# Gate weights loaded in a row, and their column sums moved, in a two-block transformer kernel (one core)

## The reference, cut to what matters

```python
mod = silu_c @ w_mod[l] + b_mod[l]
sh1, sc1, gt1, sh2, sc2, gt2 = jnp.split(mod[:, None, :], 6, axis=-1)
...
h = modulate(rms_norm_2(x, g_pre1[l]), sh1, sc1)
...
x = x + gt1 * rms_norm_2(mix, g_post1[l])
h2 = modulate(rms_norm_2(x, g_pre2[l]), sh2, sc2)
x = x + gt2 * rms_norm_2(ec_moe(h2, ...), g_post2[l])
```

## Time and profile before

| | us |
|---|---|
| median of 3 runs | 2412.12 |
| lowest, highest | 2410.62, 2414.21 |
| the profiled execution | 2412.12 |
| its span | 2410.3 |
| PE busy | 1846.0 |
| DVE busy | 528.3 |
| ACT busy | 286.5 |

### The profile page before, as it was taken

The page is one execution under the profiler, slowest core; times in us unless marked ns, Lnnn a source line. Parts: engine busy times, 40 slices in busy tenths (PEclk is TensorE's granted clock), DMA queues, the critical chain, the costliest instruction groups (busy, mean ns, idle before and its releaser), DMA issues.

```text
span 2410.3 us, 24072 instructions
## 1 busy us (share of the span) xinstructions
PE 1846.0 (77%) x10310; PEld 1025.8 (43%) x10310; DVE 528.3 (22%) x1129; ACT 286.5 (12%) x709; POOL 57.9 (2%) x95
## 2 busy tenths in 40 slices
PE   6999998999998999975766666666666666666665
PEld 3767785767785677543222222222222222222221
DVE  1244322244323337743100010000000000100001
ACT  1113211113211012311000000000000000000001
POOL 1000000000001200100000000000000000000000
PEclk9999999999999999996877787878788777887887
DMA  8843542444454231384999999999999999999997
GB/s 292 249 157 140 195 160 96 155 170 144 162 221 141 96 140 35 117 325 161 386 421 423 422 422 422 423 422 422 422 423 423 422 422 423 423 422 423 423 422 294
DMA packets 150032, 714.81 MB, mean 297 GB/s; under 512 B 11801, under 2 KB 16345, under 8 KB 96431
## 3 DMA queue, kind: packets, MB, share of 16 engines
q1 hardware_dynamic: 144064, 697.08, 72.1%
q10 hardware_dynamic: 3591, 10.29, 1.2%
q0 software_dynamic: 2272, 5.90, 1.1%
HBM read 709.43 MB, written 3.80 MB: 296 GB/s over the span
## 4 chain that ended last, share of the span: by engine, by line
PE 49%; DMA 41%; DVE 5%; ACT 1%; issue 1%; SPq 1%; POOL 0%; DVEq 0%; ACTq 0%
DMA arena<-in_w_up_dram 34%; PE banks L810 14%; PE banks L2380 6%; DMA arena<-in_w_down_dram 4%; PE banks L1663 4%; PE banks L900 3%; PE banks L1672 3%; PE banks L908 2%; PE banks L2407 2%; DMA arena<-in_w_mods_dram 2%; PE banks L815 2%; PE banks L2349 1%; PE banks L928 1%; PE banks L1705 1%; PE banks L956 1%
## 5 line engine op out<-in xcount | busy, mean ns | idle before, releaser
L2380 PE MATMUL banks<-arena 128*32 128x512 f32 (+2 forms) x3072 | 466.8, 736 | 301.3 <-DMA arena<-in_w_up_dram 295.5
L2380 PEld LDWEIGHTS banks<-arena 128*32 128x32 f32 x3072 | 127.5, 136 | 581.3 <-issue 574.7
L810 PE MATMUL banks<-arena 128*128 128x256 f32 x1536 | 344.6, 380 | 4.0 <-DMA arena<-in_w_in_dram 2.5
L810 PEld LDWEIGHTS banks<-arena 128*128 128x128 f32 x1536 | 286.7, 190 | 46.3 <-issue 4.9
L2407 PE MATMUL banks<-arena 128*32 128x512 f32 x1280 | 211.5, 795 | 121.0 <-DMA arena<-in_w_down_dram 74.8
L2520 DVE SCALAR_TENSOR_TENSOR arena<-arena,banks 64x512 f32<-64x512 f32 (+1 forms) x48 | 30.5, 635 | 780.6 <-ACT arena L2432 779.7
L2407 PEld LDWEIGHTS banks<-arena 128*32 128x32 f32 x1280 | 45.8, 129 | 266.0 <-issue 264.6
L2432 ACT ACTIVATE arena<-banks 64x512 f32<-64x512 f32 (+1 forms) x48 | 26.7, 556 | 829.3 <-PE banks L2380 823.4
L1663 PE MATMUL banks<-arena 128*128 128x256 f32 x512 | 118.9, 392 | 3.5 <-DVE arena L1991 1.9
L1663 PEld LDWEIGHTS banks<-arena 128*128 128x128 f32 x512 | 99.6, 197 | 19.0 <-issue 5.2
L2527 DVE COPY arena<-banks 128x512 f32<-128x512 f32 x16 | 11.1, 692 | 376.4 <-PE banks L2415 376.4
(11 more groups left out here) (325 smaller groups left out, 1623.9 us busy)
## 6 DMA issues: line engine op xcount, KB each, us to landing
arena<-in_w_gate_dram SPq DMA_DIRECT2D x128, 1376.0 KB, 30.1
arena<-in_w_up_dram SPq DMA_DIRECT2D x128, 1376.0 KB, 31.9
arena<-in_w_down_dram SPq DMA_DIRECT2D x160, 1024.0 KB, 30.4
arena<-in_w_in_dram SPq DMA_DIRECT2D x68, 1024.0 KB, 7.5
arena<-in_w_mods_dram SPq DMA_DIRECT2D x48, 1024.0 KB, 7.3
arena<-in_w_out_dram SPq DMA_DIRECT2D x12, 1024.0 KB, 5.7
arena<-in_w_down_dram SPq DMA_DIRECT2D x16, 512.0 KB, 21.8
arena<-in_w_o_swa_dram SPq DMA_DIRECT2D x4, 1024.0 KB, 10.9
```

Of the source, the lines that this page charges most:

```text
L810: mm = pe.matmul(b[:, i * S:i * S + S], w, rhs[:, kt, :], start=kt == 0, stop=kt == 7)
L2380: mm = pe.matmul(bank[pc][32 * g:32 * g + 32, 0:w_], xsT[:, kt, CAP * e4:CAP * e4 + CAP], (wg if g < 2 else wu)[:, c:c + w_], start=kt == ...
```

## The change

It puts all four gate loads of a stage together: in the layers behind `qb` and ahead of `kb`, in the second block behind `kn` and ahead of `vn`, and the last gate behind the four `mod` chunks. The DVE sums move with them: in the layers half 1 behind the lambda sums and half 2 behind the mean squares; in the second block both halves behind `xT2`; for the last gate half 1 behind head 1 of the scan and half 2 behind head 2. The `gate` jobs come earlier in PE's order in the layers, `gate2` comes ahead of `rk`, and `vc` 0 ahead of `v` 1. No new function is called.

```diff
     chunk("w_in", D, COL["qb"], 512)
+    for r in (0, 512):
+        for c in (4, 5):
+            loads.append(("mods_now", r, 4, 512 * c, 512))
     chunk("w_in", D, COL["kb"], 256)
-    for c in (4, 5):
-        loads.append(("mods_now", 0, 4, 512 * c, 512))
     loads.append(("w_uq", 0, 2, 0, MLA_H * QK))
     chunk("w_in", D, COL["qc"], 512)
     loads.append(("w_ukv", 0, 1, 0, MLA_H * (NOPE + VD)))
-    for c in (4, 5):
-        loads.append(("mods_now", 512, 4, 512 * c, 512))
...
     jobs += [("rotk", 0, ()), ("q", 0, uq), ("q", 1, uq), ("qc", 0, qc), ("rotq", 0, ()),
-             ("q", 2, uq), ("q", 3, uq), ("qc", 1, qc), ("rotq", 1, ()), ("kn", 0, ukv), ("kn", 1, ukv),
-             ("kc", 0, kc), ("rotq", 2, ()), ("kn", 2, ukv), ("kn", 3, ukv), ("kc", 1, kc), ("rotq", 3, ()), ("v", 0, ukv), ("v", 1, ukv), ("gate", 0, ()),
-             ("vc", 0, vc), ("gate", 1, ()), ("vc", 1, vc)]
+             ("q", 2, uq), ("q", 3, uq), ("gate", 0, ()), ("qc", 1, qc), ("rotq", 1, ()), ("kn", 0, ukv), ("kn", 1, ukv),
+             ("gate", 1, ()), ("kc", 0, kc), ("rotq", 2, ()), ("kn", 2, ukv), ("kn", 3, ukv), ("kc", 1, kc), ("rotq", 3, ()), ("v", 0, ukv), ("vc", 0, vc),
+             ("v", 1, ukv), ("vc", 1, vc)]
...
-        if name in ("kn", "vn"):
-            for c in (4, 5):
-                loads.append(("mods_now", 0 if name == "kn" else 512, 4, 512 * c, 512))
+        if name == "kn":
+            for r in (0, 512):
+                for c in (4, 5):
+                    loads.append(("mods_now", r, 4, 512 * c, 512))
+        for m in MODS_AFTER.get(name, ()):
+            for r in (0, 512):
+                loads.append(("w_mods", r, 4, 512 * m, 512))
         if name in MODS_AFTER:
             for r in (0, 512):
                 for c in (4, 5):
                     loads.append(("w_mods", r, 4, 512 * c, 512))
-        for m in MODS_AFTER.get(name, ()):
-            for r in (0, 512):
-                loads.append(("w_mods", r, 4, 512 * m, 512))
...
-    jobs += [("nv", n, i["vn"]) for n in range(2)]
+    jobs += [("nv", n, i["vn"]) for n in range(2)] + [("gate2", n, ()) for n in range(2)]
     jobs += [("rk", n, ()) for n in range(2)] + [("nv", n, i["vn"]) for n in (2, 3)]
-    jobs += [("tq", n, i["qn"]) for n in range(2)] + [("gate2", n, ()) for n in range(2)]
-    jobs += [("rq", n, ()) for n in range(2)]
+    jobs += [("tq", n, i["qn"]) for n in range(2)] + [("rq", n, ()) for n in range(2)]
...
                 nc.vector.tensor_reduce(lam[:, 0:2], th[:, 0:P].rearrange("p (a c) -> p a c", a=2), AX_X, ALU.add).then_inc(lam_sum.sem, lam_sum.up())
 
+                gate_rows(dve, GATE_LOADS, 1, l * (NLOAD // RING), 0, mrow)
                 dve.wait_ge(lam_exp.sem, lam_exp.at(l, 1))
...
+                gate_rows(dve, GATE_LOADS, 2, l * (NLOAD // RING), 0, mrow)
                 dve.wait_ge(misc_done.sem, misc_done.at(l, 2))
...
-                gate_rows(dve, GATE_LOADS, 1, l * (NLOAD // RING), 0, mrow)
                 dve.wait_ge(rows_in, 32 * l + 32)
...
-                    if n == 2:
-                        gate_rows(dve, GATE_LOADS, 2, l * (NLOAD // RING), 0, mrow)
...
             gate_rows(dve, OWN_GATE, 1, L2 * (NLOAD // RING), 1, mrow2)
+            gate_rows(dve, OWN_GATE, 2, L2 * (NLOAD // RING), 1, mrow2)
+
+            dve.wait_ge(row_in, 32)
...
+            spread_gate("gate2", G1, row2_b, row2_g)
             dve.wait_ge(lbx.sem, lbx.at(0, 1))
...
-                if kind == "rq":
-                    gate_rows(dve, OWN_GATE, 2, L2 * (NLOAD // RING), 1, mrow2)
-                    dve.wait_ge(row_in, 32)
-                    spread_gate("gate2", G1, row2_b, row2_g)
...
-            gate_rows(dve, LAST_GATE, 1, L2 * (NLOAD // RING), 1, acc2)
             for h in range(HG_H):
...
-                if h == 0:
-                    gate_rows(dve, LAST_GATE, 2, L2 * (NLOAD // RING), 1, acc2)
+                if h in (1, 2):
+                    gate_rows(dve, LAST_GATE, h, L2 * (NLOAD // RING), 1, acc2)
```

More of the change, by code:

```diff
@@ L89, in layer_jobs @@
     jobs += [("qb", 0, (i, i + 1)), ("qb", 1, (i, i + 1))]
+    i += 6
+    jobs += [("kb", 0, (i, i + 1)), ("vb", 0, (i, i + 1))]
     i += 2
[L91 to L94, removed]
+    uq, qc, ukv, kc, vc = (i,), (i + 1, i + 2), (i + 3,), (i + 4, i + 5), (i + 6, i + 7)
+    i += 8
     jobs += [("rotk", 0, ()), ("q", 0, uq), ("q", 1, uq), ("qc", 0, qc), ("rotq", 0, ()),
-             ("q", 2, uq), ("q", 3, uq), ("qc", 1, qc), ("rotq", 1, ()), ("kn", 0, ukv), ("kn", 1, ukv),
-             ("kc", 0, kc), ("rotq", 2, ()), ("kn", 2, ukv), ("kn", 3, ukv), ("kc", 1, kc), ("rotq", 3, ()), ("v", 0, ukv), ("v", 1, ukv), ("gate", 0, ()),
-             ("vc", 0, vc), ("gate", 1, ()), ("vc", 1, vc)]
+             ("q", 2, uq), ("q", 3, uq), ("gate", 0, ()), ("qc", 1, qc), ("rotq", 1, ()), ("kn", 0, ukv), ("kn", 1, ukv),
+             ("gate", 1, ()), ("kc", 0, kc), ("rotq", 2, ()), ("kn", 2, ukv), ("kn", 3, ukv), ("kc", 1, kc), ("rotq", 3, ()), ("v", 0, ukv), ("vc", 0, vc),
+             ("v", 1, ukv), ("vc", 1, vc)]
     for z in range(3):
@@ L395, in second_jobs @@
         n += 2
-        if k in ("kn", "vn"):
-            n += 2
-        if k in MODS_AFTER:
+        if k == "kn":
             n += 4
@@ L402, in second_jobs @@
             n += 2
+        if k in MODS_AFTER:
+            n += 4
     out_load = n
```

## The result

| | before | after |
|---|---|---|
| median, lowest to highest, of 4 runs each | 2413.16 (2410.62 to 2416.22) | 2433.6 (2432.55 to 2438.71) |
| the profiled execution, its span | 2412.12, 2410.3 | 2430.06, 2428.3 |
| first expert's first product | 1145.9 | 1163.6 |

The ratio is 1.0089 (95% interval 1.0069 to 1.0107), +21.5 us. The forecast was +13.6 us, 1.0056, and 2425.7 us with a range from 2418 to 2431. Slower was right, the size was too small, and the median lies above the range.

The account below looks back on a forecast made before the run. PE idle time (DVE too in the scan) was to count before 1146 us, the expert stream after. Terms 2.4 + 1.5 + 5.0 + 2.7 - 0.6 + 2.6 = +13.6 gave 2425.7 us, range 2418 to 2431.

Parts of the forecast that it names:

- What bounds the kernel: Before 1146 us only idle PE or scan DVE costs; then the expert stream, so first-expert delay passes one for one.
- (c): Rival: the expert stream swallows the delay, so a later first expert costs nothing: 2412 us, chance 0.04.
- (d): Rival: faster, because the chain's DMA pieces, 40.2 us, are the real cost: 2381 us, chance 0.03.
- Layer 1: kb starts 2.9 us late behind its load, 0.5 us of other waits go: +2.4, bounds +1.3 and +5.6.
- Layer 0: q waits for w_uq until about 90.9, qc 0 ends 2.0 later, 0.5 comes off: +1.5, bounds -1.5 and +4.
- v, and the clock behind it: Second block, before nv 0: PE waits for vn's load, +5.0, then slower matmuls at half clock, +2.7.
- gate2: Second block, gate2 ahead of rk: DVE wait -2.7, gate products +1.7, bank wait +0.35, together -0.6; bounds -3.3 and 0.
- Scan: Mod load waits go, but the last gate's DVE sums delay the scans, head 3's included: +2.6.
- the upper bound (+5): Scan: the case of later loads and a clock that falls in PE's new 4 us gap.
- The base: The sum was added to 2412.1 us, the profiled execution of the kernel before, taken as also the median.
- Rival (b): Worse: kb's gap and the scan's drop the clock too, q in layer 0 comes later: 2432 us, chance 0.06.
- rival (a): Milder: clock holds at vn or at rq, or layer 0 gains; all three 2417.3, one alone 2423; chance 0.18.

Follow-up runs that it names:

- whole_again: The changed kernel run once more, unaltered, against the kernel before: 2432.85 us, ratio 1.0070.
- clock_kept_at_nv: The whole change with 12 filler matmuls of no use in the gap before nv 0, against the kernel before: 2434.99 us, 1.0077.
- gate2_move_only: The kernel before with the two gate2 jobs moved from behind tq 1 to behind nv 3, no fillers: 2414.76 us, 0.9988.
- whole_with_fillers: The whole change with fillers both in the old kernel's waits and in the change's new gaps, against the kernel before: 2416.28 us, 1.0002.
- last_gate_only: The kernel before with only the last gate changed, loads behind the mod chunks and sums behind heads 1 and 2: 2419.74 us, 1.0019.
- small_last_sums: The whole change with the last gate's 16 DVE operations on 16 columns, not 512, against the kernel before: 2426.65 us, 1.0047.
- clock_kept_in_new_gaps: The whole change with fillers ahead of kb in layer 1, ahead of nv 0 and in the scan, against the kernel before: 2430.62 us, 1.0057.
- own_gate_only: The kernel before with only the second block's first gate changed (loads, sums, gate2 ahead of rk): 2422.75 us, 1.0032.
- fillers_only: The kernel before with fillers in nine of its old waits and gate2 where it was: 2405.77 us, 0.9948.

## Why the prediction was right in kind and too small

The 14 traces give each stretch of the change several times, with the old code and with the new (traces with fillers in the stretch left out; ahead of layer 0's scores no run has any). Means, us:

| stretch | old code (traces) | new code (traces) | difference | forecast |
|---|---|---|---|---|
| start to layer 0's first scores | 153.8 (7) | 155.6 (7) | +1.8 | +1.5 |
| layer 1, mean squares to first scores | 89.4 (7) | 91.7 (5) | +2.3 | +2.4 |
| second block, tkc to first scores | 86.7 (3) | 94.4 (4) | +7.7 | +7.1 |
| first scan product to first wo2 | 60.9 (4) | 66.9 (4) | +5.9 | +2.6 |
| sum | | | +17.7 | +13.6 |

(The old code's mean in layer 1 has three traces with fillers at the layer's start, ahead of the stretch.) In the first row single traces scatter by 5 us within the old code and by 4 within the new, so its +1.8 is known to about 1 us. The sum agrees with whole_again's +16.9. By the prediction's own steps:

*What bounds the kernel; rivals (c) and (d).* Right. From the first expert to the last product it takes 1255.7 to 1258.9 us in all 14 traces, whatever stood ahead. (c) and (d) are false.

*Layer 1.* Right. kb was in use 3.8 us after its issue, forecast 3.7, and the wait 2.97, forecast 2.9. Behind that wait kb's 16 products kept the clock in after (3.76 us), but in two of the five traces without fillers there they took 5.38, behind waits of 3.09 and 3.23.

*Layer 0.* The sum came out within the scatter, the way to it was false. "w_uq lands where that half of qc did, about 90.9, and q starts there": w_uq was not waited for. It landed at 88.5, and PE came to q at 91.57. Late was kb, which the prediction had put "inside this": 2.82 us of wait, and its 16 products took 5.20 us in place of 3.62, at half clock. qc's waits then shrank from 2.49 to 0.56 us. The cost that the prediction put on w_uq stood on kb and the clock. What it overlooked are POOL's reads of `t_rows`. They had the DMA engines until some 78 us, and the earlier kb was issued, the longer it took to its first use. In the seven traces of the new order it was issued at 73.5, 75.2, 75.5, 76.75, 76.85, 76.9 and 78.7 us and took 7.2, 5.7, 5.6, 4.9, 4.7, 5.4 and 4.0 (in the sixth the reads went on a microsecond longer); in layer 1, where POOL reads nothing, 3.8. That ACT's write would slow kb, as the prediction took from the sharing of the engines, didn't come: the write moved nothing yet. The sharing showed between POOL's reads and kb.

*v, and the clock behind it.* Right. The wait was 5.61 us, forecast 5.0; the clock cost 16.91 - 13.90 = 3.0, forecast 2.7, and clock_kept_at_nv gave it back in the trace. The Trainium skill (TensorE: Matmul & The Clock Gate, HAM oscillation) says that a long wait for a transfer between groups of matmuls makes the next group start at the low clock, and the traces agree: 5.61 us of waiting, then 0.50 of the clock.

*gate2.* The wait for DVE shrank to 3.56 (forecast 3.5). The clock still fell. The block's 7.7, less the 5.61 and the 3.0, leaves -0.9 for gate2, and gate2_move_only's -2.9 (-5.8 to 0) holds the forecast's -0.6.

*Scan: the step that failed, by its size.* Forecast +2.6, measured +4.6 (2.4 to 6.8) alone and +5.9 in the traces. What failed is that the clock behind the scan's new gaps stood at nothing in the sum. The chain on DVE was right where the clock holds: heads 2 and 3 were forecast 37.3 and 48.3 us behind the first scan product, and came at 37.2 and 47.9 in whole_with_fillers. In after they came at 38.1 and 50.1, and wo2 at 66.5. The excess over 60.4 + 2.6 is 3.5 us, in three pieces. First 0.8 us: sum 1's loads wait for mod 1, and the mod products' 32 matmuls took 5.34 us where whole_with_fillers has 3.64; there sum 1 starts 32.4 us behind the first scan product, which is the forecast's 1042.8. This piece is chance and no new gap: the wait of 2.45 us ahead of it stands in the kernel before too (2.44), and last_gate_only has 3.64 for the same products. Then 1.0: behind the 3.33 us gap L1683 and L1630 took 1.11 and 1.92 us where small_last_sums, without that gap, has 0.66 and 1.04, and DVE waits for them. Then 1.7: behind the gap of 3.09 L1634 and L1804 took 2.07 and 1.94 in place of 1.10 and 1.08. These two come back in every trace that has the sums: from head 2 to head 3 it takes 12.0 us in all four with the sums and no fillers in the scan, 11.1 and 10.7 in the two with fillers; from head 3 to wo2 16.2 to 16.4, and 14.7 in clock_kept_in_new_gaps. The prediction had named the gap and priced its clock only in the upper bound (+5), while at nv 0 it took the same effect into the sum. By its own evidence (the clock fell after 4.53 us) the gap that it forecast in the scan, 4 us, was nearly as long.

*The base.* The miss of 7.9 us is more than the sum's 4.1. The kernel before took 2412.12 in the profiled execution and 2415.4 to 2417.0 as the median of the four later sets, 3.3 to 4.9 more. Its trace says where: its first scores of layer 0 came at 152.2 where the seven traces of that code have 153.8 (150.6 to 155.9), and layer 1's stretch took 87.8, not 89.4. The clock had not fallen in the middle of the layers in that execution; own_gate_only, with the same code there, has it fall at 437 us. The sum was set on a fortunate execution, and the upper end of 2431 had no room for that. 2415.5 + 13.6 would have been 2429.1. In the first set itself, though, the kernel before had 2413.16, 1.0 more, and by that set alone the other 6.9 us belong to the change. The bounds were added up wrong besides: as stated with each term they make +2.4 to +23.0, not +2.8 to +23.6.

*Clock and waits apart.* With fillers on both sides the change costs 13.0 us (8 to 18), forecast without the clock 10.9. Without fillers it costs 16.9 to 21.5. So the fillers take back some 4 to 8 us, forecast for the clock 2.7; the intervals are too wide to say it closer. The 13.0 are not waits alone either: no fillers stand in layer 0, where kb's 16 products took 6.74 us in whole_with_fillers, and from 433 us on the clock stood at 0.50 in it for some 6 us, for some 3 in fillers_only (layer 1's stretch 93.4 and 89.4). Rival (b), that the clock falls in more gaps than one, had 0.06 and all that lies above 2431, and it is what came, apart from q in layer 0: in after it fell at kb in layer 0 (81.3), at nv 0 (825.4) and three times in the scan (1040.5, the piece that is chance, 1064.4 and 1074.6). Of rival (a) nothing came. What stays open is whether the excess of the first set over the second (21.5 and 16.9) is more than scatter.

## What to carry to other kernels

A new wait of PE costs its length and can cost the slower products behind it: here 3.0 us behind 5.61, 1.6 behind 2.82, nothing behind 2.97, and 1.8 behind 3.09 in another execution. Price both for every new gap, not only the longest. Where a forecast rests on one execution of a kernel whose clock falls at chance places, set the sum on the median of several and widen the range by their scatter. And look at what the clock already costs in the kernel as it stands: fillers in nine old waits gave 12.6 us here, where the change lost 16.9 to 21.5. Ask also, of a load that is moved, what all the other issuers have in the DMA engines at that time.

## What the runs showed of the hardware

Fillers in PE's waits made the kernel before 0.52% faster (0.35% to 0.69%), with 74 more matmuls (148 in the profile) and not one transfer less; those in layer 1 and at the end of the scan stood in waits of 1.66 to 5.95 us. The places at which the clock falls differ between executions of the same code: in layer 1, for one, it fell between 435 and 440 us in own_gate_only and gate2_move_only and not in before or last_gate_only, and all four have the same code there. The stretch to layer 0's first scores took 150.6 to 155.9 us in seven; how much of that is the clock stays open. The Trainium skill (TensorE: Matmul & The Clock Gate, What's actually happening) says that the number of slow matmuls at a kernel's start varies from run to run, and puts the cost of that start under 1% of a typical span. Here the falls in the middle of the kernel vary too, and 0.52% is what the fillers in nine waits won back.

A load that was issued while another engine's transfers had the DMA engines waited for them, although it was in another queue: kb, 1 MB in SP's queue, came into use 7.2 us after its issue when it was issued 4 to 5 us ahead of the end of POOL's reads, 4.0 when behind their end, and 3.8 in layer 1, without them. The write of na_rows is not the cause: in after its first packets moved behind 83 us, and kb was in use at 81.69. w_uq, first in SP's line 3.2 us ahead of that write, landed in 6.3 us in before; behind kb and 2.2 us ahead of the write it took 10.8 in after. How much of that is kb, the reads or the write, no run here shows.
